# Modulation as row products on VectorE, rope inside the key and value stages, and four norms applied behind the weight product, in a two-block transformer kernel

## The reference, cut to what matters

```python
# first block, layers i = 0, 1 (c and c_ctx: one vector of 1024 each)
mod_lat = silu(c) @ ada_w[i] + ada_b[i]          # ada_w[i]: 1024 x 6144
mod_ctx = silu(c_ctx) @ ada_w[i] + ada_b[i]
sh1, sc1, ga1, sh2, sc2, ga2 = split(mod_lat, 6) # context alike from mod_ctx
u = rms_norm(h, g_mix[i]) * (1 + sc1) + sh1
ql, kl, vl = split(u @ w)                        # layer 1: 4 key/value heads
ql, kl = rms_norm(ql, q_gain), rms_norm(kl, k_gain)   # per head of 64
ql, kl = apply_axial_rope(ql), apply_axial_rope(kl)   # layer 1 only
h += ga1 * attention(ql, kl, vl, context) @ w_o
h += ga2 * square(relu(modulate(rms_norm(h, g_mlp[i]), sh2, sc2) @ w1)) @ w2
# second block
u = rms_norm(h, a_norm) @ a_w_in                 # state-space layer (S5)
h += glu(gelu(s5(u)) @ a_w_glu)
h += conv_ffn(rms_norm(h, ffn_norm[0]))
k, v = split(rms_norm(h, kv_norm) @ w_kv);  k = rms_norm(k, k_norm)   # per head
q = rms_norm(rms_norm(h, b_norm) @ w_q, q_norm)
h += stick_breaking_attention(q, k, v) @ w_o
h += conv_ffn(rms_norm(h, ffn_norm[1]))
```

## Time and profile before

| | us |
|---|---|
| median of 3 runs | 1864.48 |
| lowest, highest | 1861.12, 1869.22 |
| profiled execution | 1866.02 |
| its span | 1864.0 |
| TensorE busy | 1687.1 (91%) |
| VectorE busy | 1166.4 (63%) |
| ScalarE busy | 873.8 (47%) |
| GpSimd busy | 96.7 (5%) |

### The profile page before, as it was taken

How to read it: one execution, slowest core, us unless ns; L and a number is a source line. 1 busy time by engine, 2 the same in 40 slices (tenths; PEclk the granted TensorE clock), 3 DMA queues, 4 the chain that set the end, 5 groups by cost and what they waited for, 6 DMA issues and landing times.

```text
span 1864.0 us, 36509 instructions
## 1 busy us (share of the span) xinstructions
PE 1687.1 (91%) x13158; PEld 1478.0 (79%) x13158; DVE 1166.4 (63%) x1960; ACT 873.8 (47%) x1517; POOL 96.7 (5%) x152
## 2 busy tenths in 40 slices
PE   5899999799999989688979998788999888779999
PEld 3678767687878777574779998688999877579999
DVE  5775485643224456758767777666876575557774
ACT  4564485343113322464554554254555466445553
POOL 0001120000000012100000203100000000000000
PEclk9999999899999999897989999898999889889999
DMA  9246441354344355330146657734556434025564
GB/s 369 104 169 226 177 131 63 119 192 145 139 167 165 140 188 191 111 113 1 47 165 200 207 188 235 281 114 128 188 180 203 147 108 152 1 91 186 184 194 146
DMA packets 79684, 291.46 MB, mean 156 GB/s; under 512 B 10000, under 2 KB 11792, under 8 KB 77408
## 3 DMA queue, kind: packets, MB, share of 16 engines
q1 hardware_dynamic: 69120, 248.96, 38.7%
q0 software_dynamic: 10464, 41.15, 6.8%
HBM read 271.39 MB, written 18.68 MB: 156 GB/s over the span
## 4 chain that ended last, share of the span: by engine, by line
PE 73%; DVE 14%; ACT 6%; issue 4%; DMA 2%; SPq 1%; DVEq 0%; POOL 0%; ACTq 0%
PE bank L604 20%; PE bank L605 20%; PE bank L606 20%; PE bank L514 2%; DVE stat L1770 2%; ACT w_hi L1001 1%; PE bank L664 1%; PE bank L666 1%; PE bank L665 1%; PE bank L675 1%; DVE w_lo L1373 1%; DVE prob L1789 1%; PE bank L781 1%; DMA ada_first<-ada_w 1%; PE bank L792 1%
## 5 line engine op out<-in xcount | busy, mean ns | idle before, releaser
L604 PE MATMUL bank<-u_hi,w_hi 128*128 128x256 f32 (+1 forms) x1936 | 618.4, 319 | 58.8 <-DVE u_lo L1584 29.7
L605 PE MATMUL bank<-u_lo,w_hi 128*128 128x256 f32 (+1 forms) x1936 | 606.5, 313 | 0.0
L606 PE MATMUL bank<-u_hi,w_lo 128*128 128x256 f32 (+1 forms) x1936 | 605.7, 313 | 0.0
L1373 DVE TENSOR_TENSOR w_lo<-raw,w_hi 128x1024 fp32r<-128x1024 f32 x372 | 453.7, 1223 | 240.9 <-ACT w_hi L1001 226.6
L1001 ACT ACTIVATE w_hi<-raw 128x1024 fp32r<-128x1024 f32 x360 | 377.0, 1050 | 211.5 <-PE bank L606 186.8
L604 PEld LDWEIGHTS bank<-u_hi,w_hi 128*128 128x128 f32 x1936 | 378.9, 196 | 90.0 <-issue 66.5
L605 PEld LDWEIGHTS bank<-u_lo,w_hi 128*128 128x128 f32 x1936 | 379.0, 196 | 19.9 <-issue 2.2
L606 PEld LDWEIGHTS bank<-u_hi,w_lo 128*128 128x128 f32 x1936 | 378.4, 195 | 18.7
L604 PE MATMUL bank<-hid_hi,w_hi 128*128 128x512 f32 (+1 forms) x512 | 176.1, 344 | 5.7 <-ACT hid_hi L1047 5.7
L605 PE MATMUL bank<-hid_lo,w_hi 128*128 128x512 f32 (+1 forms) x512 | 173.1, 338 | 0.0
L606 PE MATMUL bank<-hid_hi,w_lo 128*128 128x512 f32 (+1 forms) x512 | 173.1, 338 | 0.0
(11 more groups left out here) (286 smaller groups left out, 2329.6 us busy)
## 6 DMA issues: line engine op xcount, KB each, us to landing
raw<-weights SPq DMA_DIRECT2D x372, 512.0 KB, 3.8
ada_raw<-ada_w SPq DMA_DIRECT2D x80, 512.0 KB, 6.1
ada_first<-ada_w SPq DMA_DIRECT2D x16, 512.0 KB, 15.6
bias_sb<-bias_na POOLq DMA_DIRECT2D x16, 256.0 KB, 3.2
toep_dram<-zeros POOLq DMA_DIRECT2D x8, 512.0 KB, 8.9
bat_dram<-bat POOLq DMA_DIRECT2D x16, 256.0 KB, 3.3
ca_dram<-ca POOLq DMA_DIRECT2D x16, 256.0 KB, 4.4
s_bat<-bat_dram POOLq DMA_DIRECT2D x4, 1024.0 KB, 5.1
```

Of the source, the lines that this page charges most:

```text
L604: pe.matmul(dst, wh, hi[:, kt, xs], start=first, stop=False)
L605: pe.matmul(dst, wh, lo[:, kt, xs], start=False, stop=False)
L606: return pe.matmul(dst, wl, hi[:, kt, xs], start=False, stop=final)
L1373: TT(w_lo[:, slot, :], raw[:, slot, :], w_hi[:, slot, :].bitcast(F32), ALU.subtract).then_inc(S["lo"], 1)
```

## The change

Three edits.

**Modulation.** The 80 later blocks of ada_w are stored transposed, so that a partition holds the 1024 weights of one output column. silu(c) and silu(c_ctx) are spread over all partitions once at the start (`silu_rows`: eight products with the identity for each, on TensorE; `silu_row_copy`, on ScalarE). Then VectorE multiplies a unit by that row and writes out the sum (`ada_unit`): twice a unit for blocks 16 to 63, once from 64 on. After four units it adds the bias. No modulation is left on TensorE after the start. The plan says how many units each stage's weight unit takes along (`ada`). Two buffers hold the units, and SP loads each two units ahead.

**Rope.** Four permutation products stand between k1 and v1, four behind v1's first tile and two behind its second, in banks 6, 7, 4, 5; VectorE combines four before v1 and the others in v1's tiles.

**Norms behind the product.** down1b and fdown0 prepare the operand of the next stage without the norm's factor: `u_hi` and `u_lo` of `h` times the gain, made block by block as `h` gets ready (`next_hi`, `next_lo`). The row total goes into the first tile of win and of k2. The factor is applied to the results: win's tiles are multiplied by it on VectorE on their way out; k2 and q2, which have a norm for each head anyway, put it in the per-head norm's small term (`late_mean`, `late_root`, `late_scale`); v2's copy on ScalarE is scaled with it by column. The norms a, kv and b are gone. win, k2 and q2 are written out tile by tile instead of in a loop of four.

The core of the diff, in which `a1`, `d1` and the like are the steps of a tile that ScalarE (a) and VectorE (d) report:

```diff
-        Stage("qk0", "QK", 16, tok=TOK, ada=(0, 16)),
-        Stage("v0", "V", 8, tok=TOK, ada=(0, 32)),
-        Stage("wo0", "RES", 8, tok=TOK, ada=(0, 40), norm=True, gate=(0, 2)),
-        Stage("up0a", "MLP", HALF, tok=TOK, ada=(1, 0)),
-        Stage("down0a", "RES", 8, units=2, tok=TOK, ada=(1, 16), gate=(0, 5)),
-        Stage("up0b", "MLP", HALF, tok=TOK, ada=(1, 24)),
-        Stage("down0b", "RES", 8, units=2, tok=TOK, ada=(1, 40), norm=True, gate=(0, 5)),
+        Stage("qk0", "QK", 16, tok=TOK, ada=(0, 1) * 8),
+        Stage("v0", "V", 8, tok=TOK, ada=(1,) * 8),
+        Stage("wo0", "RES", 8, tok=TOK, ada=(1,) * 8, norm=True, gate=(0, 2)),
+        Stage("up0a", "MLP", HALF, tok=TOK, ada=(0, 1) * 8),
+        Stage("down0a", "RES", 8, units=2, tok=TOK, ada=(1,) * 16, gate=(0, 5)),
+        Stage("up0b", "MLP", HALF, tok=TOK, ada=(1, 2) * 8),
+        Stage("down0b", "RES", 8, units=2, tok=TOK, ada=(1,) * 8 + (0,) * 8, norm=True, gate=(0, 5)),
...
+        Stage("down1b", "RES", 8, units=2, norm=True, gate=(1, 5), prep=(("a", 0),)),
+        Stage("win", "IN", 8, late="a"),
...
+        Stage("fdown0", "RES", 8, units=3, norm=True, prep=(("kv", 0), ("b", SEQ))),
+        Stage("k2", "QK", 8, late="kv"),
...
+        Stage("q2", "QK", 8, late="b"),
...
+            def load_ada(a):
+                if a >= FIRST_ADA + 2:
+                    sp.wait_ge(S["ada_read"], a - 1)
+                sp.dma_start(ada_raw[:, a % 2, :], ada_w[a]).then_inc(ada_in[a % 2], 16)
...
+            def silu_rows(c):
+                pe.wait_ge(row_copied, c) if c else pe.wait_ge(silu_d, 1)
+                for kt in range(KT):
+                    mm = pe.matmul(ROW_BANKS[kt // 4][:, kt % 4 * P:(kt % 4 + 1) * P],
+                                   silu_pad[:, kt, c:c + 1].to_broadcast([P, P]), C("ident"), start=True, stop=True,
+                                   skip_group_check=True)
+                mm.then_inc(row_made, 1)
...
+                if s.name in PREPARED:
+                    made, sets, k = PREPARED[s.name]
+                    pe.wait_ge(S["ul"], value("ul", ST[made], sets * kt + k + 1))
...
+                        if t == 5 and rows is not None:
+                            row_total(rows)
...
+            def rope_turn(m):
+                if m >= 4:
+                    pe.wait_ge(rope_d, m - 3)
+                elif m >= 2:
+                    pe.wait_ge(S["d2"], value("d2", ST["k1"], 2))
+                else:
+                    pe.wait_ge(S["d2"], value("d2", ST["q1"], 8))
+                dst = q1[:, m, :] if m < 8 else k1[:, m - 8, 0:SEQ]
+                pe.matmul(psum[(6, 7, 4, 5)[m % 4]][:, 0:SEQ], C("perm"), dst, start=True,
+                          stop=True).then_inc(rope_p, 1)
...
-                def modulation(i):
-                    pe.wait_ge(S["ada_copy"], value("ada_copy", s, i * 1))
-                    for slot in range(4):
-                        pe.wait_ge(ada_in[slot], i * 16 + 16 * (s.base["ada"] // 4 - 3))
-                    ada_body([ada_raw[:, slot, :] for slot in range(4)], ADA_PART)
...
+                        gemm_tile(s, i, jj, body, rows=None if jj else rows)
+                        if name == "v1":
+                            for m in (range(4, 8), range(8, 10))[jj]:
+                                rope_turn(m)
...
+                elif name in LATE and name != "q2":
+                    one(0, NORM_AFTER[LATE[name]])
...
+            for m in range(4):
+                rope_turn(m)
+            gemm("v1"); drained("v1"); drained("q1"); drained("k1")
...
-            gemm("up1b"); copied("up1b"); gemm("down1b"); table_kernel(7, 0); row_total("down1b"); drained("down1b")
...
+            gemm("up1b"); copied("up1b"); gemm("down1b"); table_kernel(7)
             gemm("win"); drained("win")
...
-            gemm("fup0"); gemm("fdown0"); row_total("fdown0"); drained("fdown0")
+            gemm("fup0"); gemm("fdown0")
...
                     A(sq[:, b2, 0:s.tok], bank[:, 0:s.tok], ACT.Square).then_inc(S["a1"], 1)
-                    if jj:
+                    if s.name in LATE:
+                        A(QK_DST[s.name][:, bass.ds(j, 1), 0:s.tok].rearrange("p a t -> p (a t)"), bank[:, 0:s.tok],
+                          ACT.Copy).then_inc(S["a3"], 1)
+                        if j:
+                            late_root(s, j - 1)
...
+                            if s.name == "v2":
+                                for t in range(2):
+                                    last = A(val2[:, t, cols], src[:, t, :], ACT.Copy, scale=col_y[:, 2 * t:2 * t + 1])
...
+            def next_hi(s, j, k):
+                prep = s.more.get("prep", ())
+                if k < len(prep):
+                    name, c0 = prep[k]
+                    A(u_hi[:, bass.ds(j, 1), c0:c0 + SEQ].rearrange("p a t -> p (a t)"),
+                      h[:, bass.ds(j, 1), 0:SEQ].rearrange("p a t -> p (a t)"), ACT.Copy,
+                      scale=late_gain(name, j)).then_inc(S["uh"], 1)
...
+            def late_root(s, j):
+                b2 = (s.tile0 + j) % 2
+                act.wait_ge(S["dv"], value("dv", s, j + 1))
+                act.wait_ge(S["d2"], value("d2", s, j - 1))
+                y = rs[:, b2, 0:s.tok]
+                chain.link(root(y, tmp[:, b2, 0:s.tok]))
+                A(late_y2[:, b2, :], y, ACT.Square).then_inc(S["a2"], 1)
...
+            def ada_unit(a):
+                layer, m = divmod(a, N_ADA)
+                b, conds = a // 4 % 2, 2 if a < BOTH_ADA else 1
+                raw_ = ada_raw[:, a % 2, :]
+                if a == FIRST_ADA:
+                    dve.wait_ge(row_copied, 2)
+                dve.wait_ge(ada_in[a % 2], 16 * ((a - FIRST_ADA) // 2 + 1))
+                if conds == 2:
+                    dve.wait_ge(S["ada_read"], a)
+                    STT(ADA_DUMP, raw_, 1.0, silu_row[:, 1, :], ALU.mult, ALU.mult, accum_out=ada_acc[:, b, a % 4, 1:2])
+                STT(raw_, raw_, 1.0, silu_row[:, 0, :], ALU.mult, ALU.mult,
+                    accum_out=ada_acc[:, b, a % 4, 0:1]).then_inc(S["ada_read"], 1)
+                if a % 4 == 3:
+                    dve.wait_ge(S["ada_read"], a + 1)
+                    ms = slice(m - 3, m + 1)
+                    TT(mod[:, layer, ms, 0:conds], ada_acc[:, b, :, 0:conds], adab[:, layer, ms, 0:conds],
+                       ALU.add).then_inc(S["mod"], 1)
...
+                elif s.kind == "IN":
+                    dve.wait_ge(S["unit"], n_done)
+                    TT(u_sc[:, i, :, jj, :], bank[:, 0:SEQ].rearrange("p (c s) -> p s c", s=CH),
+                       rsn[:, 0:SEQ].rearrange("p (c s) -> p s c", s=CH), ALU.mult).then_inc(S["d1"], 1)
...
+            def next_lo(s, j, k):
+                prep = s.more.get("prep", ())
+                if k < len(prep):
+                    name, c0 = prep[k]
+                    n = j * len(prep) + k
+                    dve.wait_ge(S["uh"], value("uh", s, n + 1))
+                    STT(dcol(u_lo, j, slice(c0, c0 + SEQ)), dcol(h, j, slice(0, SEQ)), late_gain(name, j),
+                        dcol(u_hi, j, slice(c0, c0 + SEQ)).bitcast(F32), ALU.mult, ALU.subtract).then_inc(S["ul"], 1)
...
+            def late_mean(s, j):
+                b2 = (s.tile0 + j) % 2
+                dve.wait_ge(S["p2"], value("p2", s, j + 1))
+                dve.wait_ge(S["d2"], value("d2", s, j - 1))
+                STT(tmp[:, b2, 0:s.tok], (SS, SS2)[b2][:, 0:s.tok], -0.5 * INV_HD, rsn[:, 0:s.tok], ALU.mult,
+                    ALU.add).then_inc(S["dv"], 1)
+            def late_scale(s, j):
+                b2 = (s.tile0 + j) % 2
+                dst = QK_DST[s.name][:, j, 0:s.tok]
+                dve.wait_ge(S["a2"], value("a2", s, j + 1))
+                dve.wait_ge(S["a3"], value("a3", s, j + 1))
+                v, y, y2_ = tmp[:, b2, 0:s.tok], rs[:, b2, 0:s.tok], late_y2[:, b2, :]
+                link(TT(v, v, y2_, ALU.mult))
+                link(STT(dst, dst, VC(QK_GAIN[s.name][0], j + QK_GAIN[s.name][1]), y, ALU.mult, ALU.mult))
+                STT(dst, v, 1.5, dst, ALU.add, ALU.mult).then_inc(S["d2"], 1)
```

More of the change, by code:

```diff
@@ L61, in increments @@
     c = {"unit": n * s.units}
-    if s.kind == "QK":
+    if s.kind == "QK" and s.more.get("late"):
+        c.update(a1=n, a3=n, p2=n, dv=n, a2=n, d2=n)
+    elif s.kind == "QK":
         c.update(a1=n, d1=n, p2=n, a2=n, d2=n)
     elif s.kind == "IN":
-        c.update(a1=n)
+        c.update(d1=n)
     elif s.kind == "V":
@@ L77, in increments @@
         c.update(d1=n // 2, d2=n // 2, a2=n // 2, a3=n // 2, d3=n // 2, sq=1)
-    if s.ada is not None:
-        c.update(ada=n, ada_copy=n // 4, ada_sum=n // 4, mod=n // 4)
+    sets = len(s.more.get("prep", ()))
+    if sets:
+        made = n // 2 if s.kind == "GLU" else n
+        c.update(uh=made * sets, ul=made * sets)
+    if s.ada:
+        c.update(ada_read=sum(s.ada), mod=sum(s.ada) // 4)
     return c
@@ L399, in pair_slice, with turns @@
```

(26 more changed lines are left out.)

288 lines of the change are left out of this document (172 added, 116 removed).

## The result

| | before | after |
|---|---|---|
| median, us | 1866.21 (4 runs, 1861.12 to 1869.22) | 1816.8 (4 runs, 1814.17 to 1817.9) |
| ratio | | 0.9734, 95% interval 0.9715 to 0.9754 |
| span of the profiled execution | 1864.0 | 1816.0 |
| TensorE, VectorE, ScalarE busy | 1687.1, 1166.4, 873.8 | 1634.7, 1306.3, 865.6 |

The kernel is 49.4 us faster (2.7%), where 57 were forecast; 1816.8 lies 9 us above the forecast and inside the range.

A forecast was written before the change was run, and what follows sets the result against it. TensorE was taken as the bound in the MLP of layer 0, with stops between stages elsewhere. Modulation -30.4, rope 0, win -6.8 and k2/v2/q2 -19.4 sum to -57 us: 1808, own range 1797 to 1822, eight in ten 1790 to 1838.

The forecast's parts named there:

- Price of a product: VectorE's row product over 128x1024 with its sum written out, taken as 1.3 us, next to the maximum.
- Rival 1: The VectorE product costs double, 2.4 us, and is open wherever VectorE or the loop binds: 1878 us; chance 0.10.
- Hidden in the MLP: In up0a, down0a and up0b VectorE's products stay hidden behind TensorE: -9.6, -4.8 and -9.6 us.
- qk0 and v0: VectorE becomes the bound; its cost and a later start offset six modulation bodies, 14.3 us: sum 0, from -4 to +5.
- wo0: One loop of engines decides, 6.3 us a tile against 5.43 on TensorE alone; 49.5 us, as now: 0.
- down0b: Products hide beside the tables: -4.8 us; TensorE's 1.61 us wait for mod goes as well; loads cost nothing.
- Rope: Moved into key and value stages; attention would start at 852.6 against 852.15 us: 0, from -5 to +4.
- win: Norm moved behind win: stops around the total go, transposes come earlier, down1b slows; sum -6.8 us.
- rival 2: The gain at win is hidden by transfers, since tables 2 and 3 follow win's end: 1816 us; chance 0.10.
- The 3.4 us behind win: Transposes after win start 3.4 us late; this goes because weight loads are asked for before the tables: -3.4 us.
- The table stretch: After win, tables 2 and 3 are asked for early and queue on the same engines: 1 us lost.
- k2, v2, q2: Stop after fdown0 goes, k2 tiles run in a 4.0 us loop: -19.8 us, q2 +0.4; sum -19.4.

## Why the prediction was right or wrong

- **Price of a product: right.** 1.3 was taken; the two records make 1.30 to 1.37, and they hold the queue for 1.14 to 1.26. Rival 1 (twice the price) is out: a sum written out does not halve the rate. By the Trainium skill, Vector Engine (DVE) Microarchitecture Reference, Points that are easy to get wrong, this form runs at half the throughput; as an estimate, from the elementwise 1.22 us, that would be 2.4 us. No row of this case shows it, with the sum or without.
- **Hidden in the MLP: right.** up0a, down0a and up0b have the same length without any product. The small shortfall in up0a (8.5 for 9.6) is not theirs, since it stays when they go.
- **qk0 and v0: the sum right, with some luck.** 0 forecast with the start, 0.1 measured. The products cost 9.1 us there, where the prediction's terms (21 - 17 + 7) make 11, and the start 1.9 where 3 was taken. The six bodies were worth 11.0 us and not 14.3: without any product the two stages take 160.3, before 171.3. So two errors of about 3 us cancel. VectorE is the bound, as forecast, though at 18.5 of 20 us and not above 19.
- **wo0: too low by 1.7 us.** The loop of h, square, w_hi, w_lo and two products is the bound as the prediction says (5.9 us open), but the row total behind it waits 8.09 us, where it waited 2.73, and then itself runs at the lower clock (2.08 us, where it took 1.12 before). To its total the stage is 0.75 us longer than before, and 0.95 from there on.
- **down0b: the step that failed.** Forecast -6.4, measured -2.3. By pieces: to the first table's turn +3.1 us, from there to the last small kernel -6.2, from that kernel to the norm's total +1.8, the total and norm -1.1. The middle piece is the forecast's gain, bodies and the wait for mod of the earlier trace rows together. The first is a cost that the prediction put at nothing ("DMA: ... Nothing"): the stage begins with a stop for table inputs, 4.79 us before and 7.90 after. It counted the loads, which are as many as before, and not what else is in flight where they are issued. With the units of ada_w out of down0b and the issue in its old place the stop is 5.47, without any product 5.51; how loads and products share the 3 us stays open. The third is a wait put in place of another: TensorE no longer waits for mod ahead of the last kernel, but then 1.78 us for ssum behind it, as VectorE is the later one there (the total's row: 739.76, idle 1.78 for ssum).
- **Rope: right in size, the mechanism half named.** The tail is not shorter; the 2 us are the clock at the start of attention, which stood in the prediction as a possible gain. The rest of its working holds: v1 begins 60.5 us behind q1, where 832.5 stood for 60.0.
- **win: the term that was mis-sized, and rival 2's mechanism.** From down1b to glu -6.8 was forecast and -2.8 measured; the edit by itself is worth some 2.8. By pieces: win's start is 3.8 us nearer to down1b's, win itself as long as before (27.9 us), and from the transposes to glu 1.1 longer.
  - The start came as forecast (-6.9 + 2.8 + 0.6 = -3.5), though not in the way named: win does not begin at once. down1b's tiles take 6.5 to 6.7 us, so the last table input `ca` comes later, and TensorE stops 2.67 us for it ahead of the last small kernel. That kernel and win's first products run at the lower clock (0.50), where the prediction had counted on 1.2 us back:

```profile
1119.89 0.76 DVE L1971 SCALAR_TENSOR_TENSOR ca<-ca,tab_tmp 128x576 f32<-128x576 f32 x1
```

```profile
1120.70:1123.70 3.00, 3.00 (x41) 2.55 (x42) 2.94 (x6) 1.48 (x6) 0.75 (x1) 0.50 0.76 239
```

  - The 3.4 us behind win are the term that failed. The transposes still wait 3.16 us, 3.36 before, behind a weight load of 11.81 us. The reason given for its going was that the weights would be asked for before the tables. GpSimd issues the six table loads from 1132.23 to 1134.90, and that weight load goes out at 1134.84.
  - The table stretch cost 1.1 us, against the 1 forecast. TensorE waits there 10.84 us in one piece for s_bat, a load that is issued only when a buffer has been read, where 1.02 and 2.33 stood before. Most of that is no loss: from the end of those products to glu it takes 17.2 us, 21.8 before; the wait of 2.42 us for VectorE's h_high, for one, is gone. With the rope put back the wait for s_bat is shorter, 7.65 us, and the stretch longer, 45.0 us against 43.0.

```profile
1134.84 11.81 DMA raw<-weights
1155.79 12.27 DMA s_bat<-bat_dram
```

- **k2, v2, q2: right, number and mechanism.** -19.3 for -19.8 up to q2, +0.6 for +0.4 in it. k2 and v2 take 33.2 and 24.3 us, where 32.9 and 24 were worked out. The loop's pace was forecast as 4.0 us a tile. ScalarE's timeline of k2 has the high parts of three successive units 3.9 us apart:

```profile
1456.40 1.04 ACT L1078 ACTIVATE w_hi<-raw 128x1024 fp32r<-128x1024 f32 x1
1460.28 1.04 ACT L1078 ACTIVATE w_hi<-raw 128x1024 fp32r<-128x1024 f32 x1
1464.17 1.04 ACT L1078 ACTIVATE w_hi<-raw 128x1024 fp32r<-128x1024 f32 x1
```

By time alone rival 2 (1816) came closer than the forecast, but its own step explains 4 of the 9 us and down0b 4; the rest nearly cancels. Of the signs that the prediction named, three did not come: VectorE above 19 of 20 us in qk0, under 1.5 us of idle time and no clock of 0.50 between down1b and win, and the transposes 7 us earlier (3.9).

## What to carry to other kernels

Work moved off the busiest engine costs nothing only where three things have room: the engine that takes it, the loop of engines that it is put into, and the transfers in flight at that place; check the third where a stage begins with loads of its own. A stop taken away ahead of a stage counts in full only up to the next wait for a load; a gain forecast behind that wait needs its own reason, so follow the order in which the loads are issued. An idle time that grew is not yet a cost: compare the length of the whole stretch. Here a wait grew from 3.4 to 10.8 us and the stretch by 1.1. Once work is divisible in units, spread it by what each stage has free: four units moved from qk0 to v0 made the two stages 6.3 us shorter.
